# One 512-column matmul for the high and low parts of x in the gate and up projections, with the halves added by VectorE

## What is computed

```
# first block (twice)
ffn = (jax.nn.silu(x @ w_ffn_gate[l]) * (x @ w_ffn_up[l])) @ w_ffn_down[l]
x = layer_norm(ALPHA * x + ffn, ln2_g[l], ln2_b[l])
# second block (twice): the gate is first convolved over three tokens per feature, then GELU
x = x + (gelu(conv3(h @ w_ffn_gate, conv_w) + conv_b) * (h @ w_ffn_up)) @ w_ffn_down
```

## Time and profile before

| | us |
|---|---|
| median of three executions (lowest to highest) | 1945.11 (1943.42 to 1949.39) |
| the profiled execution, device time | 1949.93 |
| its span, first to last instruction | 1948.1 |

### The profile page before, as it was taken

The page is one execution under the profiler, slowest core; times in us unless marked ns, Lnnn a source line. Parts: engine busy times, 40 slices in busy tenths (PEclk is TensorE's granted clock), DMA queues, the critical chain, the costliest instruction groups (busy, mean ns, idle before and its releaser), DMA issues.

```text
span 1948.1 us, 30829 instructions
## 1 busy us (share of the span) xinstructions
PE 1828.9 (94%) x11794; PEld 1657.5 (85%) x11794; DVE 1152.1 (59%) x1634; ACT 935.2 (48%) x1576; POOL 438.3 (22%) x184
## 2 busy tenths in 40 slices
PE   7899989998899989999989998999888999989996
PEld 7797779998897779997878998999777889989995
DVE  5764454446674554446567486666565765866664
ACT  6433244445533244446554555444574545554444
POOL 2240112221250012221251112222122411212221
PEclk8995699998896689999999999999989999999998
DMA  9420146654410145654532345555445222646652
GB/s 331 132 66 1 63 151 186 190 183 134 155 63 22 39 158 187 184 184 140 185 119 76 113 135 185 181 183 193 156 133 183 87 98 82 201 145 195 186 185 89
DMA packets 78634, 276.74 MB, mean 142 GB/s; under 512 B 8687, under 2 KB 11416, under 8 KB 78504
## 3 DMA queue, kind: packets, MB, share of 16 engines
q1 hardware_dynamic: 75224, 271.43, 43.1%
q10 hardware_dynamic: 3280, 3.47, 0.7%
HBM read 273.81 MB, written 1.06 MB: 141 GB/s over the span
## 4 chain that ended last, share of the span: by engine, by line
PE 63%; DVE 7%; ACT 2%; issue 2%; POOL 0%; ACTq 0%; DVEq 0%
PE bank L633 29%; PE bank L647 22%; PE bank L1041 2%; PE bank L1068 2%; PE bank L663 1%; DVE w_lo L600 1%; PE bank L1049 1%; PE bank L791 1%; PE bank L781 1%; PE bank L872 1%; PE bank L864 1%; ACT sq L1333 1%; PE bank L863 0%; PE bank L1081 0%; DVE merged L2175 0%
## 5 line engine op out<-in xcount | busy, mean ns | idle before, releaser
L600 POOL TENSOR_TENSOR w_lo<-raw,w_hi 128x1024 fp32r<-128x1024 f32 x146 | 361.1, 2474 | 1444.6 <-ACT w_hi L596 1444.6
L600 DVE TENSOR_TENSOR w_lo<-raw,w_hi 128x1024 fp32r<-128x1024 f32 x364 | 520.3, 1446 | 275.6 <-ACT w_hi L596 274.6
L596 ACT ACTIVATE w_hi<-raw 128x1024 fp32r<-128x1024 f32 x510 | 529.0, 1053 | 297.1 <-PE bank L633 148.7
L633 PE MATMUL bank<-x_t_hi,w_hi 128*128 128x256 f32 x2112 | 608.9, 288 | 2.9 <-issue 2.9
L633 PE MATMUL bank<-x_t_lo,w_hi 128*128 128x256 f32 x2112 | 601.8, 285 | 0.0
L633 PE MATMUL bank<-x_t_hi,w_lo 128*128 128x256 f32 x2112 | 601.5, 285 | 0.0
L633 PEld LDWEIGHTS bank<-x_t_hi,w_hi 128*128 128x128 f32 x2112 | 409.0, 194 | 9.1 <-issue 5.8
L633 PEld LDWEIGHTS bank<-x_t_lo,w_hi 128*128 128x128 f32 x2112 | 408.8, 194 | 3.7 <-issue 0.5
L633 PEld LDWEIGHTS bank<-x_t_hi,w_lo 128*128 128x128 f32 x2112 | 408.2, 193 | 0.0
L647 PE MATMUL bank<-w_hi,x_t_hi 128*128 128x512 f32 (+3 forms) x384 | 136.4, 383 | 0.7 <-issue 0.7
L647 PE MATMUL bank<-w_lo,x_t_hi 128*128 128x512 f32 (+3 forms) x384 | 134.3, 377 | 0.0
(11 more groups left out here) (367 smaller groups left out, 2507.2 us busy)
## 6 DMA issues: line engine op xcount, KB each, us to landing
raw<-stream SPq DMA_DIRECT2D x511, 512.0 KB, 4.3
x<-x_in SPq DMA_DIRECT2D x1, 1024.0 KB, 6.2
bias_r<-rev_dram ACTq DMA_DIRECT2D x1, 1024.0 KB, 11.7
pe_t<-pe ACTq DMA_DIRECT2D x4, 256.0 KB, 2.8
y_out<-x SPq DMA_DIRECT2D x1, 1024.0 KB, 4.1
param<-param ACTq DMA_DIRECT2D x2, 289.0 KB, 3.0
bias_r<-rev_dram ACTq DMA_DIRECT2D x1, 512.0 KB, 4.1
consts<-consts SPq DMA_DIRECT2D x1, 500.0 KB, 10.9
```

What stands on the lines that cost most here:

```text
L596: self.eng.activation(w_hi[:, i, :], raw[:, i, :], ACT.Copy).then_inc(hi_done.sem, 1)
L600: self.eng.tensor_tensor(w_lo[:, i, :], raw[:, i, :], w_hi[:, i, :].bitcast(F32), ALU.subtract).then_inc((lo_pool if self.part == "pool" e ...
L633: mm = pe.matmul(target, a[:, i, w], b[:, k0 + kt, :], start=kt + k == 0, stop=3 * kt + k == n - 1)
```

## The change

`x_t_hi` and `x_t_lo` become the two planes of one tensor `x_t`, so that a moving operand of 2 x 256 columns can take both for one kt. A new function `feature_wide` runs a gate or up unit: for each kt one matmul of 512 columns with w_hi (w_hi by x high into the left half of the bank, w_hi by x low into the right half) and one of 256 columns with w_lo into the left half. Each gate and each up has a whole bank now (`ga{i}`, `ub{i}`, over the same four banks). VectorE adds the two halves of each bank by a `tensor_reduce` with two inputs for each of 256 outputs, into new SBUF tensors `gate_sum` and `up_sum`, which frees the bank. Silu, the convolution and the product read those. In the second block the gate's halves are added, and the convolution is made, without waiting for the up unit. ScalarE waits for the product by a counter of its own (`hidden`). Other uses of `x_t_hi` and `x_t_lo`, and the down units, stay.

```diff
@@ banks: both tables
-    ... *[f"gu{i}" for i in range(FT)])
+    ... *[n for i in range(FT) for n in (f"ga{i}", f"ub{i}")])
@@ tensors
-        x_t_hi = sb("x_t_hi", [P, KT, S], F32R)
-        x_t_lo = sb("x_t_lo", [P, KT, S], F32R)
+        x_t = sb("x_t", [P, 2, KT, S], F32R)
+        x_t_hi, x_t_lo = x_t[:, 0], x_t[:, 1]
...
+        gate_sum = sb("gate_sum", [P, 2, S], at=hgrn + 5 * one)
+        up_sum = sb("up_sum", [P, 2, S], at=hgrn + 5 * one + one // 2)
@@ TensorE
+            def feature_wide(at, name, u, arrive=None):
+                pe.wait_ge(*banks.free(at, name))
+                use_unit(at, u)
+                b, i = bank[banks.bank(at, name)], u % RING
+                both = b[:].rearrange("p (a s) -> p a s", a=2)
+                for kt in range(KT):
+                    if arrive and kt % 2 == 0:
+                        pe.wait_ge(*banks.read(at, f"{arrive}{kt // 2}"))
+                    w = slice(kt * P, (kt + 1) * P)
+                    first = pe.matmul(both, w_hi[:, i, w], x_t[:, :, kt, :], start=kt == 0, stop=False)
+                    if kt == 0:
+                        first.then_inc(unit_begun.sem, 1)
+                    mm = pe.matmul(b[:, 0:S], w_lo[:, i, w], x_t[:, 0, kt, :], start=False, stop=kt == KT - 1)
+                mm.then_inc(*banks.fills(at, name))
@@ feed_forward
-                        name = f"gu{i}"
-                        pe.wait_ge(*banks.free(at, name))
-                        b = bank[banks.bank(at, name)]
-                        feature_major(at, uid[f"gate{i}"], b[:, 0:S], x_t_hi, x_t_lo, KT,
-                                      arrive="yt" if i == 0 else None)
-                        feature_major(at, uid[f"up{i}"], b[:, S:2 * S], x_t_hi, x_t_lo, KT
-                                      ).then_inc(*banks.fills(at, name))
+                        feature_wide(at, f"ga{i}", uid[f"gate{i}"], "yt" if i == 0 else None)
+                        feature_wide(at, f"ub{i}", uid[f"up{i}"])
@@ ScalarE, first block
-                    act.wait_ge(*banks.full(at, f"gu{i}"))
-                    act.activation(gs[:, i % 2, :], bank[banks.bank(at, f"gu{i}")][:, 0:S], ACT.Silu
+                    act.wait_ge(*banks.read(at, f"ga{i}"))
+                    act.activation(gs[:, i % 2, :], gate_sum[:, i % 2, :], ACT.Silu
                                    ).then_inc(c["gate_silu"].sem, 1)
-                    act.wait_ge(*banks.read(at, f"gu{i}"))
+                    act.wait_ge(*c["hidden"](at, i + 1))
@@ VectorE
+            def add_halves(at, name, target):
+                dve.wait_ge(*banks.full(at, name))
+                dve.tensor_reduce(target, bank[banks.bank(at, name)][:].rearrange("p (a s) -> p s a", a=2), AX.X, ALU.add
+                                  ).then_inc(*banks.frees(at, name))
@@ VectorE, first block
                     split.ahead(uid[f"up{i}"])
+                    if i >= 2:
+                        dve.wait_ge(*c["gate_silu"](at, i - 1))
+                    add_halves(at, f"ga{i}", gate_sum[:, i % 2, :])
+                    add_halves(at, f"ub{i}", up_sum[:, i % 2, :])
+                    dve.wait_ge(*banks.read(at, f"ub{i}"))
                     dve.wait_ge(*c["gate_silu"](at, i + 1))
...
-                    dve.tensor_tensor(hs[:, i % 2, :], gs[:, i % 2, :], bank[banks.bank(at, f"gu{i}")][:, S:2 * S], ALU.mult
-                                      ).then_inc(*banks.frees(at, f"gu{i}"))
+                    dve.tensor_tensor(hs[:, i % 2, :], gs[:, i % 2, :], up_sum[:, i % 2, :], ALU.mult
+                                      ).then_inc(c["hidden"].sem, 1)
@@ VectorE, second block
                     split.ahead(uid[f"up{i}"])
-                    dve.wait_ge(*banks.full(at, f"gu{i}"))
+                    add_halves(at, f"ga{i}", gate_sum2[:, i % 2, :])
+                    dve.wait_ge(*banks.read(at, f"ga{i}"))
...
-                    g, v, w = bank[banks.bank(at, f"gu{i}")][:, 0:S], cv[:, i % 2, :], par2("conv")[:, 3 * i:3 * i + 3]
+                    g, v, w = gate_sum2[:, i % 2, :], cv[:, i % 2, :], par2("conv")[:, 3 * i:3 * i + 3]
...
+                    add_halves(at, f"ub{i}", up_sum2[:, i % 2, :])
+                    dve.wait_ge(*banks.read(at, f"ub{i}"))
                     dve.wait_ge(*c["gate_silu"](at, i + 1))
...
-                    dve.tensor_tensor(hs2[:, i % 2, :], gs2[:, i % 2, :], bank[banks.bank(at, f"gu{i}")][:, S:2 * S],
-                                      ALU.mult).then_inc(*banks.frees(at, f"gu{i}"))
+                    dve.tensor_tensor(hs2[:, i % 2, :], gs2[:, i % 2, :], up_sum2[:, i % 2, :], ALU.mult
+                                      ).then_inc(c["hidden"].sem, 1)
```

10 lines of the change are left out of this document (6 added, 4 removed).

## The result

The change makes the kernel slower by 1%. The medians are 1967.44 us after (1961.47 to 1968.80, 4 runs) and 1947.25 us before (1943.42 to 1949.72, 4 runs), a ratio of 1.0095 with a 95% interval of 1.0074 to 1.0115. The forecast was 1928.8. The profiled execution took 1968.80 us with a span of 1967.0 us, 18.9 us above the span in the earlier trace rows.

The account below looks back on a forecast made before the run. TensorE, busy nearly throughout the four feed-forward stages, was taken as the bound. Its saving of 16.3 us, with VectorE's additions hidden and edges at 0, took the median from 1945.1 to 1928.8 us, range 1924 to 1938.

Parts of the forecast that it names:

- Part 1, TensorE's stream: Gate and up units in all four feed-forward stages: eight matmuls fewer a unit save 93 ns, 16.3 us over 176 units.
- Rival A: Gate and up matmuls: a second operand run or switching operand shapes eats the saving, time up to 1945; chance 0.05.
- Part 2, the additions: VectorE, two reduces a tile of 512 inputs and 256 outputs: 0.69 us each, 121 us of work outside TensorE's stream.
- Part 2, VectorE's round in the second block: VectorE's in-order chain per second-block tile: 7.8 us against TensorE's 8.32, so VectorE follows with 0.5 us to spare.
- the term for GpSimd: Second-block VectorE round: 0.3 us added for low parts taking 1.78 beside GpSimd's and convolution and product operands in SBUF.
- Part 3, edges: Ends of the second block's stages, last tile's hs_lo wait: change put at 0, between -1.5 and +2 us for both.
- Rival B: Second block: VectorE becomes the bound if a reduce doubles to 1.38 us; round 9.2 us, time 1959; chance 0.07.
- Rival C: Steady state holds, but stage ends, GpSimd's SBUF share or a late ring return 3 to 8 us: 1932-1937; chance 0.07.
- Rival E: TensorE's fixed part is the price of changing between w_hi and w_lo; nothing saved, time stays at 1945; chance 0.03.
- The prediction's argument against it: Down units: pairs of matmuls share an operand yet start 228 ns apart one by one, 10 starts in 2.28 us.
- D: TensorE's stream: weight loads bound it, so the change doesn't do what it says; given no chance of its own.
- the first block's cover: First block: VectorE's work grows from 3.7 to 5.1 us of TensorE's 8.32 a tile, so the additions are easily hidden.

Follow-up runs that it names:

- The layout in one run: Changed kernel with x_t laid out so the 512 columns of the moving operand lie in one run: 1966.75 us, ratio 1.0089 to before.
- the grouped kernel: Changed kernel, all second-block feed-forward low parts on VectorE, each gate/up unit's 8 512-column matmuls ahead of its 8 of 256: 1935.64 us, 0.9936 of before.
- GpSimd's instruction cut short: Changed kernel, GpSimd making only 64 of 1024 columns of its low parts in the second block's feed-forward: 1944.18 us, 0.9969 of before.
- the kernel without GpSimd: Changed kernel with all low parts of the second block's feed-forward made by VectorE, none by GpSimd: 1942.70 us, 0.9966 of before.

## Why the prediction was wrong, point by point

**Part 1, TensorE's stream.** The mechanism was right, and its size was off by half. The prices of a 512 and of a 256 matmul stood for streams of one width each, and the sum put them in a stream that changes width at every step. That costs 5.3 ns a pair (353.1 for 347.8), and there are 1408 pairs: 7.5 us of the 16.3. Rival A named this doubt, as a switch between operands of two shapes, beside that of a second run, and its sign came: 236 ns behind a 512-column matmul in gate and up units, 228 to 232 in down units. The layout in one run cleared the second run, and the grouping showed that the alternation is what costs. Grouping takes away the changes of width and most changes between `w_hi` and `w_lo` at once, so it doesn't tell these two apart by itself. But before has as many changes between the weights at one width, and there a matmul starts 119.7 ns behind one with the same weights and 120.0 behind one with the others: the change of weights holds 0.3 ns. The Trainium skill (TensorE: Matmul & The Clock Gate, Back-to-back issue gap) gives N/2.4 + 2.5 ns as the gap of an isolated matmul, and says that in a stream the loads of the weights set the spacing too. The prediction's estimate from it, 2.5 ns saved for a matmul less, did not hold here: the grouped kernel saves 85 ns a unit for its 8 matmuls, 10.6 ns each.

**Part 2, the additions.** 0.69 us predicted, 0.683 measured. The row chosen as nearest was the right one.

**Part 2, VectorE's round in the second block.** This is the step that failed. The base was right: a round with two low parts and nothing beside it was put at 7.3 us; with GpSimd's instruction cut short such a round took 6.94. Wrong was the term for GpSimd. The prediction read the 1.78 us in the earlier trace rows as the price of a low part beside GpSimd's, spread that and put 0.3 us on the round for the operands moved to SBUF. But 1.78 was no price. GpSimd's instruction in the earlier trace rows ends at 746.53 + 2.40 = 748.93, and VectorE's at 748.23 + 1.78 = 750.01, 1.08 later: the duration says how much of GpSimd's instruction was left when VectorE began. Another meeting, with more of it left, costs more, up to 1.4 us each time. The rows given held this hint, by adding start and duration on both engines, and the other meetings in before's trace, with 0.5 to 1.5 us left and the same 1.08 at the end, bear it out. Moreover the change itself made the meetings longer: from 1204 to 1382 VectorE's low parts have a mean of 1613 ns after and 1468 before, where one alone takes 1230, though 12 of them stall in FF2a in both kernels. It moved the conv's first step from the bank, where 44 of 44 took 0.53 to 0.55 us, to SBUF, where it can stall. And with VectorE late, the units are all there when ScalarE comes to them: it makes three `w_hi` in one go (1251.00 to 1253.94), where in before the third stood apart and waited for the bank at 1255.04. GpSimd and VectorE then get their low parts at the same time. The round came to 8.78 us and not 7.8, with the additions at their predicted price.

The Trainium skill states this rule, and the prediction passed it by. SBUF — State Buffer, section SBUF: two separate sides (Who interferes with whom), has it that VectorE and GpSimd share one port pair, which is locked for a whole instruction, and that a VectorE instruction with two SBUF inputs, beside a GpSimd one that reads SBUF, or in a mode with two ports, takes part in it. The traces agree: the low part waits (2.66 us for 1.23) and so does the conv's first step (1.77 for 0.41), the reduce from the bank does not (0.69).

**Part 3, edges.** Put at 0 with +2 us at most for two stages; it was 4.5 us more waiting and 2.5 us of lower clock in each, less 1.4 behind the last matmul. Without the stall the term was about right: in the kernel without GpSimd the last wait is 1.57 us for 0.74, in both stages. Being late is not a loss spread over the tiles, it is collected at the stage's end, and there it is made dearer by the clock that the wait takes away.

**Rival B** had the place (VectorE's in-order chain), the sign and nearly the size: 1959 for a round of 9.2 us, against 1967 for one of 8.78. But its trigger was a reduce of twice the price, which did not come, so its nearness is luck. TensorE waited in 9 of 22 tiles of FF2a and not in every one. It also set off some 8 us of lead in the two stages against the loss. A lead of VectorE's only decides when TensorE begins to wait; it is gone by the end of the stage, where the last `hs_lo` is as late as VectorE is. **Rival C** named GpSimd's share of the SBUF, which is the cause, and priced it at 3 to 8 us back in all. **Rival E** gave no saving at all, since the changes between `w_hi` and `w_lo` stay as many; the tile went from 8.50 to 8.41 us with just as many, so it is out. (The prediction's argument against it held too, though the earlier trace rows shows its ten starts merged in twos: in the trace the single starts there are 227 to 231 ns apart in the mean of each kind.) So is D, by the grouped kernel's 2.79 us a unit. Banks, transfers, the count of 1408 matmuls and the first block's cover were as predicted.

**The sum again.** In the four stages -16.3 us was forecast and +15.7 measured, 32 us apart. Of these, 7.5 are the alternation. The stall makes 4.00 + 5.23 - 0.74 = 8.5 us of waits in a second-block stage, 2.4 of restarts behind them and 2.5 at the lower clock, less 1.4 at its end: 12.0, and twice that is 24.0. The rest of 0.5 us, and the 3.2 us of the untouched stretches, are within what executions of the same instructions differ by.

## What to carry to other kernels

Where VectorE and GpSimd work side by side, add start and duration on both: instructions of VectorE that end at a fixed distance behind GpSimd's are stalls, and their mean duration is no price to build a sum on. Moving an operand from PSUM to SBUF can put an instruction into that contest, and giving the helper's work to the engine that sets the pace can then be the faster choice. A price from a uniform stream holds for a uniform stream, so keep matmuls of one width together, and count the lateness of a pipelined engine at the end of the stage, where nothing hides it.

## What the runs showed of the hardware

- A VectorE `tensor_tensor` or `scalar_tensor_tensor` whose inputs both lie in SBUF, or a float32 `tensor_scalar` from SBUF to SBUF, that begins while GpSimd runs a `tensor_tensor` in SBUF ends a fixed time behind GpSimd's, whatever was left of it: 1.08 us for 1024 elements, 0.28 for 256, and 0.15 for 256 in the `tensor_scalar` (to 0.01). One that began up to 1.0 us before GpSimd's instruction is not slowed. A `tensor_reduce` that reads PSUM runs through at 0.68 to 0.69 us beside it, and in before so did the `tensor_scalar` that read PSUM (0.53 to 0.55).
- 512-column and 256-column fp32r matmuls in turn take 353 ns a pair (236 and 117); eight and eight in runs take 230 and 119 ns each, and the change between two such runs costs nothing. A change of weights at one width costs 0.3 ns. Whether the 512 columns are one run of SBUF or two 8 KB apart makes no difference.
- A reduce of 512 inputs to 256 outputs costs 683 ns with its pairs 1 KB apart in the bank, no more than one with neighbours.
- After 5.23 us of waiting TensorE restarted at 1.2 GHz (426 ns for 512 columns) and stayed there for its 12 matmuls.
- Stretches of unchanged instructions differ by up to 5.7 us between before and after, and by as much between executions of one program's stretch (249.78 to 255.12), with the time at the lower clock, which is as much as the smaller effects here. So an effect below 0.3% of this kernel is read from the stage it is in, not from the total.
